# First attention of a two-block layer: scores and both groups' compressed scores issued ahead of the gate's part in the even steps

## What is computed

```python
# per query tile (block_fn)
dist = t[:, None] - c_end[None, :]
s = einsum('bgrqd,bgcd->bgrqc', qc, kc) + shared_bias(dist)      # compressed scores, 31 per head
p_cmp = masked_softmax(s, dist >= 0)
o_cmp = einsum('bgrqc,bgcd->bgrqd', p_cmp, vc)
# selected blocks and window: each 128 queries against up to 512 keys, one softmax a head
s = einsum('bgrqd,bgqkd->bgrqk', qc, kb) + group_bias(dist)
o_slc = einsum('bgrqk,bgqkd->bgrqd', masked_softmax(s, ...), vb)
# ... the window branch alike
# beside it, independent products of the block's input h with w_in:
y_a = (y_a * silu(g_nsa)) @ w_proj_a
y_b = (y_b * silu(g_lru)) @ w_proj_b
m = sigmoid(gate_a) * y_a + sigmoid(gate_b) * y_b
```

## Time and profile before

| | |
|---|---|
| three runs | 1289.54, 1291.94 (median), 1301.94 us |
| profiled execution | 1288.83 us, of which the span is 1287.0 us |
| granted TensorE clock, mean | 0.983 |
| busy PE / DVE / ACT / POOL | 1218.3 / 560.8 / 306.6 / 250.3 us |
| weight loads (PEld) | 692.4 us |

### The profile page before, as it was taken

The page is one execution under the profiler, slowest core; times in us unless marked ns, Lnnn a source line. Parts: engine busy times, 40 slices in busy tenths (PEclk is TensorE's granted clock), DMA queues, the critical chain, the costliest instruction groups (busy, mean ns, idle before and its releaser), DMA issues.

```text
span 1287.0 us, 13575 instructions
## 1 busy us (share of the span) xinstructions
PE 1218.3 (95%) x5056; PEld 692.4 (54%) x5056; DVE 560.8 (44%) x1433; ACT 306.6 (24%) x725; POOL 250.3 (19%) x221
## 2 busy tenths in 40 slices
PE   7999999999999999999999899999999999988885
PEld 3555444454544444588884446766664564433342
DVE  3257384377645421208982367512223543222221
ACT  5202644433310000223022245300000321110110
POOL 7000022354510000070610030311300021211100
PEclk9999999999999999999999999999999999998988
DMA  9949104224264103313132102202239499999995
GB/s 302 219 156 240 66 6 127 82 84 146 66 214 130 66 18 130 127 53 131 66 110 87 56 11 66 71 0 66 66 143 380 182 344 398 407 401 406 410 411 173
DMA packets 94951, 212.85 MB, mean 165 GB/s; under 512 B 20125, under 2 KB 54317, under 8 KB 83063
## 3 DMA queue, kind: packets, MB, share of 16 engines
q1 hardware_dynamic: 81360, 190.51, 40.7%
q0 software_dynamic: 10320, 18.80, 5.9%
q10 hardware_dynamic: 3200, 2.61, 0.7%
HBM read 205.20 MB, written 14.75 MB: 171 GB/s over the span
## 4 chain that ended last, share of the span: by engine, by line
PE 71%; SPq 9%; DVE 7%; DMA 6%; ACT 2%; issue 2%; POOL 2%; POOLq 0%; DVEq 0%; ACTq 0%
PE PS L2336 8%; SPq L2879 7%; PE PS L1035 6%; PE PS L1464 4%; PE PS L2399 4%; PE PS L1544 4%; PE PS L1727 4%; PE PS L1729 4%; PE PS L2507 3%; PE PS L3011 3%; PE PS L1473 2%; DMA AN<-in_w_down 2%; DMA AN<-scr_line 2%; PE PS L1785 2%; PE PS L662 2%; PE PS L1773 2%
## 5 line engine op out<-in xcount | busy, mean ns | idle before, releaser
L1035 PE MATMUL PS<-HT,W 128*128 128x512 f32 x256 | 123.5, 605 | 1.8 <-ACT AN L1199 1.7
L1298 POOL TENSOR_SCALAR AN<-AN,SM 128x128 f32<-128x128 f32 (+3 forms) x64 | 72.4, 1138 | 231.6 <-DVE SM L1401 231.6
L1332 DVE SCALAR_TENSOR_TENSOR AN<-AN,COLA 128x256 f32<-128x256 f32 x168 | 86.0, 512 | 5.7 <-DMA AN<-in_w_ada 0.6
L3011 PE MATMUL PS<-AN,HT 128*64 128x512 f32 x192 | 61.6, 632 | 10.6 <-DMA X<-in_w_up 6.4
L1035 PEld LDWEIGHTS PS<-HT,W 128*128 128x128 f32 x256 | 44.1, 192 | 38.6 <-issue 35.0
L3096 DVE TENSOR_TENSOR HT<-HT,PS 128x256 f32<-128x256 f32 x16 | 6.7, 421 | 130.2 <-ACT HT L3071 130.2
L1464 PE MATMUL PS<-HT,W 128*128 128x512 f32 x128 | 57.5, 597 | 0.0
L2507 PE MATMUL PS<-W,AN 128*128 128x512 f32 x128 | 57.1, 595 | 0.0
L1279 ACT ACTIVATE AN<-PS,SM 128x128 f32<-128x128 f32 (+3 forms) x64 | 33.6, 525 | 93.8 <-DVE SM L1380 93.5
L2399 PE MATMUL PS<-AN,W 128*128 128x512 f32 x128 | 55.7, 593 | 0.1
L1544 PE MATMUL PS<-W,AN 128*128 128x512 f32 x128 | 55.4, 592 | 0.0
(11 more groups left out here) (522 smaller groups left out, 2321.7 us busy)
## 6 DMA issues: line engine op xcount, KB each, us to landing
W<-in_w_in SPq DMA_DIRECT2D x13, 2048.0 KB, 8.2
W<-in_w_down SPq DMA_DIRECT2D x20, 1024.0 KB, 27.8
AN<-in_w_gate SPq DMA_DIRECT2D x17, 1024.0 KB, 25.2
AN<-in_w_up SPq DMA_DIRECT2D x17, 1024.0 KB, 27.4
AN<-in_w_ada SPq DMA_DIRECT2D x16, 1024.0 KB, 6.2
AN<-in_w_down SPq DMA_DIRECT2D x12, 1024.0 KB, 26.6
W<-in_w_in SPq DMA_DIRECT2D x11, 1024.0 KB, 7.7
W<-in_w_gate SPq DMA_DIRECT2D x10, 1024.0 KB, 23.7
```

The source lines that it names most:

```text
L1035: t = pe.matmul(u.ap, w[:, c, tile(m)], hT[:, c, :], start=c == 0, stop=c == 7)
L1298: pool.tensor_scalar(PU[u % 5][:, 0:n], PU[u % 5][:, 0:n], RSUM[:, u:u + 1], None, ALU.mult).then_inc(*sc_pool.up(u))
L1332: dve.scalar_tensor_tensor(out=a, in0=wt[:, c, :], scalar=ca["c2"][:, c:c + 1], in1=a, op0=ALU.mult, op1=ALU.add).then_inc(*ada_dve.up(p, c))
L3011: t = pe.matmul(u.ap[r, :].rearrange("p (n f) -> p n f", n=2), XGT[e % 2][:, c, r], w_gu(3 * e + half)[:, c], start=c == 0, stop=c == 7)
```

## The change

Three edits, in `pe_compressed`, `pe_attention` and `dve_compressed`. First, in each even step PE issues the scores, then the compressed part, then the gate part, then the transpose; before it was gate part, compressed, scores, transpose. In odd steps, where there are no scores, the compressed part comes ahead of the gate part too. Second, the compressed scores of both groups are issued in x = 4, alternating between the groups, group 1 into one of banks 0 to 2 and group 0 into bank 6 as before; the step x = 5 has none any more. Third, DVE's two subtractions both stand in x = 4. Nothing is added to or taken from the number of matmuls, and the orders on ACT, POOL and SP stay as they are.

```diff
@@ pe_compressed
-        if 0 <= ph < 2:
-            pr = slice(64 * ph, 64 * ph + 64)
-            u = B.take(6, 7, "cs", i, ph)
-            wp.wait_ge(*u.free)
+        if ph == 0:
+            u = [B.take(6, 7, "cs", i, 0), B.take(0, 3, "cs", i, 1)]
+            wp.wait_ge(*u[0].free)
+            wp.wait_ge(*u[1].free)
             wp.wait_ge(*B.use("qT", 3).out)
             wp.wait_ge(*B.use("kcT").out)
             for r in range(4):
-                t = pe.matmul(u.ap[:, r * 31:(r + 1) * 31], QT[pr, r, tile(i)], KCT[pr, :], start=True, stop=True)
-            t.then_inc(*u.filled)
+                for g in range(2):
+                    pr = slice(64 * g, 64 * g + 64)
+                    t = pe.matmul(u[g].ap[:, r * 31:(r + 1) * 31], QT[pr, r, tile(i)], KCT[pr, :], start=True, stop=True)
+                    if r == 3:
+                        t.then_inc(*u[g].filled)
@@ pe_attention: moved behind the scores, with pe_compressed ahead of the gate parts
-            if step < 16:
-                pe_gate(pe, wp, "gn", 3, step // 4, step % 4)
...
-            pe_compressed(pe, wp, *divmod(step, 16))
             if step < NU and step % 2 == 0:
...
+            pe_compressed(pe, wp, *divmod(step, 16))
+            if step < 16:
+                pe_gate(pe, wp, "gn", 3, step // 4, step % 4)
...
@@ dve_compressed
-        if 0 <= ph < 2:
-            u = B.use("cs", i, ph)
+        if ph == 0:
+            for g in range(2):
+                u = B.use("cs", i, g)
...
```

## The result

The changed kernel takes 1316.49 us (median of 4 runs, 1314.99 to 1317.97) against 1291.08 for the kernel before (4 runs, 1289.54 to 1301.94): ratio 1.018, with a 95% interval of 1.0148 to 1.0213. It is slower by some 25 us, where +11 was forecast, and it lies above the range, whose top was 1309. The sign was right, the size was not.

What follows compares the result with a forecast made beforehand. PE was taken as the bound from 200.82 us on; savings −1.6 − 3.0 and losses +4.9 + 1.0 + 6.6 + 3.1 gave +11.0 on 1288.8, so 1299.8, median put at 1301.5; forecast 1294 to 1307 (0.68), wider range 1289 to 1309.

Steps and rivals of the forecast that it cites:

- (4): Step 18: the gate part no longer runs ahead of the wait for the Silu, +1.7 us, net +1.0.
- Term (2): Compressed scores of both groups run side by side: 1.0 us saved a tile, 3.0 us for tiles 1 to 3.
- Term (3): Next gate tile's first part waits for ACT's copy out of bank 7 in listed steps from 20 to 60: +4.9 us.
- Term (5): Score bank lent to the compressed scores: waits for exponentials at steps 22, 38, 52 and 54, +6.6 us.
- Term (6): Steps 32 to 36, the second Silu: scores and compressed scores wait ahead of the gate part, +3.1 us.
- some 13: Sign in the trace after: PE's waits at scores and compressed scores for ACT's exponential grow from 4.0 us to this.
- rival (C): Waits feed each other in some 10 pairs, or TensorE's clock falls in step 36's standstill: 1305 to 1315 us; chance 0.12.
- steps 20 and 6: nothing: At these two steps the bank lent to the compressed scores was said to cost no wait.
- (A): Rival: only the savings come, waits for bank 7, lent bank and steps 32 to 36 vanish: 1284 to 1290 us; chance 0.12.
- (B): Rival: nothing moves, as DVE leads all over and hides savings and losses: 1288 to 1293 us; chance 0.08.
- A change of the array's shape: Going to another array shape costs 0.12 us; one fewer in 13 even steps from 20 on saves 1.6 us.

Runs made afterwards that it cites:

- with the waits filled: The changed kernel with 17 products of 128x512, whose result is overwritten, added where PE stood waiting for an exponential; 1304.73 us, ratio 1.0095 to the kernel before.
- and odd steps' old order: The changed kernel with the 17 added products and the gate part ahead of the compressed part again in odd steps; 1304.39 us, ratio 1.007.
- the second: The changed kernel with the gate part put back ahead of the scores in every step, paired compressed scores and lent score bank kept; 1293.62 us, ratio 1.0015.
- fifth: The changed kernel with the gate part ahead of the scores again and group 1's compressed scores in a transposes' bank, 3 or 4; 1289.41 us, ratio 0.9988.
- the last experiment: The kernel before with scores and compressed scores ahead of the gate part only at step 36, no bank lent; 1298.22 us, ratio 1.004.
- the ninth: The changed kernel, gate part ahead of the scores, group 1's compressed scores in a transposes' bank, 5 overwritten products added at steps 7 and 18; 1289.13 us, ratio 0.9971.
- the experiment on bank 7: The changed kernel with the gate part ahead of the scores only in nine steps where a gate tile gets its last part; 1311.16 us, ratio 1.0147.

## Why the prediction was wrong

The shifts beside each other, in us. The forecast's column adds its own terms up to the step:

| after step | forecast | changed kernel | with the waits filled | and odd steps' old order |
|---|---|---|---|---|
| 16 | −0.7 | 6.1 | 1.8 | 0.9 |
| 35 | 2.2 | 6.7 | 3.4 | 2.5 |
| 38 | 6.4 | 14.4 | 7.5 | 6.6 |
| 51 | 7.3 | 15.7 | 8.6 | 7.7 |
| 54 | 10.3 | 21.5 | 10.9 | 10.0 |
| 55 | 10.3 | 24.6 | 12.5 | 9.9 |
| 67 | 11.0 | 25.1 | 13.1 | 10.5 |

**The terms of the sum** that were priced held, but for (4). Term (2), the pair: 16 records take 208.64 to 209.65, 1.01 us, in the changed kernel, as worked out, and where no wait interferes the shift falls by 1.0 to 1.4 at step x = 5 of a tile, as the second and fifth experiments show. Term (3), bank 7: 0.47 us and the open weight load, 0.6 to 0.7 in all in tile 1, 0.6 in tile 2, 0.5 in tile 3, against 0.72, 0.61 and 0.50; the list of steps had left out step 48. Term (5), the lent bank: 0.71 us at step 22 (0.8 forecast), 2.17 at 38 (2.2), 1.12 at 52 (1.2), 1.90 at 54 (2.4, or 2.5 by its own 318.9 − 316.4). Term (6), with the pair: 2.2 us from step 35 to 37 at full clock, against 3.1 − 1.0. Here are step 20 and the start of the next gate tile, which answer to the earlier trace rows:

```profile
208.06 0.70 PE L1118 MATMUL PS<-AN 64*128 64x256 f32 x4
208.64 1.08 PE L1052 MATMUL PS<-SM,AN 64*128 64x31 f32 x16
209.65 1.98 PE L1035 MATMUL PS<-HT,W 128*128 128x512 f32 x4
...
212.32 1.98 PE L1035 MATMUL PS<-HT,W 128*128 128x512 f32 x4 [0.47 <-ACT AN L1211]
```

Adding these waits up without taking anything off was right from step 18 on: with the clock kept up and the odd steps as the sum had them, the shift rises from 1.2 there to 10.5, by 9.2 us against 10.0. Up to step 18 the agreement is luck. Term (4) had −0.7 us and then +1.7, net +1.0; what came is +0.9 from the first tile and only 0.3 at step 18, net 1.2, because PE reached the wait for the Silu late. So 10.5 against 11.0 is closer than the sum deserves. PE's waits for exponentials at scores and compressed scores are 18.0 us (16.2 + 1.8), where "some 13" was named; those of steps 6 and 14, 3.25 and 3.09, were not in it.

**What failed first: the clock.** The prediction kept it for rival (C), at step 36 only, with a chance of 0.12 for the whole rival. Its reason against was a granted clock of 1.00 in a stretch where PE idled "1.4 of 20 us, though in short pieces". That stretch had no wait of the length that the sum itself had just worked out (2.2, 2.4, 3.1 us). The kernel before does have one of 3.04 us, and its clock stayed up there in the execution that was profiled; one execution is no proof, as the same wait of 3.04 us cost 1.6 to 2.3 us in the profiled executions of the second, the fifth and the last experiment. The changed kernel has seven stretches at 1.2 GHz in the attention. The price is 12 us of 25: the shift falls from 25.1 to 13.1 with the waits filled. The Trainium skill (TensorE: Matmul & The Clock Gate, Part 1) says that the throttled state is the default and that activity releases it, which agrees with the fills.

**What failed second: the odd steps.** The diff moves the compressed part ahead of the gate part there too, and the section on the change says so. The sum was worked with the gate part ahead. That uncovers the transposes' wait at step 55, 2.66 us where it was 0.94, and one at step 7: 2.6 us (13.1 to 10.5).

**What failed third: "steps 20 and 6: nothing".** Step 6 was put at nothing without a reason beside it; the prediction's first paragraph has DVE setting the pace there and PE with slack, and step 14 is not named at all. The wait at step 6 is 3.25 us, PE comes late with its transposes, and DVE, which waits for some of them, is busy 17.78 of 20 us instead of 19.04. After step 16 the shift is 0.9 us with the waits filled and the odd steps' old order, where −0.7 was forecast. The odd steps make it 1.8 and the clock 6.1, since steps 6 and 14 each have a wait of over 3 us; here is step 6:

```profile
164.38 0.80 PE L1118 MATMUL PS<-AN 64*128 64x128 f32 x4 [3.25 <-ACT AN L1283]
165.11 3.32 PE L1035 MATMUL PS<-HT,W 128*128 128x512 f32 x4
```

Where PE was idle for 1.4 us in 20, an order that makes it lose 3 us at once is not hidden by DVE.

**The rivals.** (A) fell as argued: PE waits for the copies at eleven places. (B) fell: DVE did not lead. (C) was nearest, with 1316.49 just above its 1305 to 1315. It came by its second half (the clock, which it had at step 36 alone) and not by its first (other steps waiting too): no step without a worked-out wait lost more than 0.1 us at full clock, but for those named above.

## What to carry to other kernels

Work that needs nothing belongs ahead of an instruction that may wait, not behind it: here 1.8 us of gate part ahead of the scores covered seven long waits, bank 7's turnaround and a lent bank all at once, and the same pair of compressed scores that cost nothing measurable with that cover was part of a loss of 1.8% without it. When a sum on TensorE comes to new waits of 2 to 3 us, price each once more for what runs behind it at half clock (1.4 to 2.8 us a wait here where the clock fell): one trace of before, in which it stayed up behind such a wait, is no proof that it will. A bank taken from a ring of three is paid by the next user of the ring, so ask which bank comes free soonest and who stands behind it.

## What the runs showed of the hardware

In the changed kernel the granted clock fell to 1.2 GHz around or behind seven waits of PE of 1.1 to 3.3 us in which PE ran nothing, and went back up while PE worked on; a gate part in such a stretch took 2.6 to 3.6 us instead of 1.8. Not every such wait did this: in the same execution 2.49 us at step 18 were followed by full clock, and so were 2.65 us at step 55 of the kernel with the waits filled. Useless products in the waits kept it at 2.4 GHz through the attention in all three traces that have them at these waits (the fourth, the ninth and the eleventh experiment): 17 of them made a kernel of 1316 us 12 us faster. 4 of them made the kernel before 0.2% faster (0.9976, 0.996 to 0.9993), of which there is no trace to read.

The same wait of 3.04 us at step 18 was followed by a gate part of 1.72 us in the profiled execution of the kernel before and of 3.13 us in that of the last experiment, whose instructions are the same up to there (3.4 us in the second and the fifth). The wait of 1.12 us at step 52 was followed by 3.44 us in the changed kernel and 1.82 in the experiment on bank 7. What decides between them was not settled.

A change of the array's shape cost about what was read: the step pairs of tile 1 without a wait and without ada (26 to 28, 30 to 32) are shorter by 0.15 us in the changed kernel, where the sum had 0.12 for the one such change that the new order saves.
